# Two-block transformer on one core: three weight tiles of the second token tile fetched during the first, and the order of the expert-row slots

## The reference

```python
# end of the first block
h = rms_norm(x, norm_ffn_g[l]) * (1.0 + sc2) + sh2
x = x + gt2 * (jnp.square(jax.nn.relu(h @ ffn_w1[l])) @ ffn_w2[l])
# second block
h = h + hybrid_mixer(rms_norm_2(h, norm_mix_g[l]), w_in[l], ...)
h = h + peer_ffn(rms_norm_2(h, norm_ffn_g[l]), w_peer_q[l], ...)
# peer_ffn, per token: the rows of 8 x 16 experts
hval = jnp.einsum('cd,chkd->chk', xc, expert_u[ic])
a = gc * jax.nn.gelu(hval, approximate=False)
y = jnp.einsum('chk,chkd->cd', a, expert_v[ic])
```

## Time and profile before

| | |
|---|---|
| median of 3 runs | 1539.07 us (1538.23 to 1541.64) |
| profiled execution, its own time | 1537.54 us |
| its span | 1536.2 us |
| TensorE busy | 1236.7 us, 81% of the span |
| VectorE busy | 937.5 us, 61% |
| ScalarE, GpSimd busy | 395.7 us (26%), 378.5 us (25%) |
| bytes moved | 488.51 MB, of these 268.45 MB by the gathers (q0), 215.55 MB by SP's queue (q1) |
| chain that ended last | TensorE 45%, DMA 28%, DVE 17% |

### The profile page before, as it was taken

The page is one execution under the profiler, slowest core; times in us unless marked ns, Lnnn a source line. Parts: engine busy times, 40 slices in busy tenths (PEclk is TensorE's granted clock), DMA queues, the critical chain, the costliest instruction groups (busy, mean ns, idle before and its releaser), DMA issues.

```text
span 1536.2 us, 14325 instructions
## 1 busy us (share of the span) xinstructions
PE 1236.7 (81%) x4974; PEld 764.9 (50%) x4974; DVE 937.5 (61%) x2022; ACT 395.7 (26%) x1043; POOL 378.5 (25%) x285
## 2 busy tenths in 40 slices
PE   2989999979999899877777756786489777788775
PEld 2875555654676685477445454433284332333332
DVE  6278877945111221156766779998668777767653
ACT  2162111121100222112212132343214433333322
POOL 0001121200000000023333323434237544444430
PEclk9999999979999898987888879879689999989999
DMA  9633334525588665749999999999999999999995
GB/s 365 242 145 123 124 136 165 195 108 190 233 333 342 228 260 188 285 187 422 424 424 424 424 420 422 366 389 423 401 358 387 421 421 421 421 420 422 420 422 218
DMA packets 56233, 488.51 MB, mean 318 GB/s; under 512 B 6496, under 2 KB 8800, under 8 KB 10080
## 3 DMA queue, kind: packets, MB, share of 16 engines
q0 software_dynamic: 36864, 268.45, 42.4%
q1 hardware_dynamic: 18144, 215.55, 35.9%
q10 hardware_dynamic: 1152, 3.59, 0.6%
HBM read 486.51 MB, written 1.05 MB: 317 GB/s over the span
## 4 chain that ended last, share of the span: by engine, by line
PE 45%; DMA 28%; DVE 17%; issue 4%; ACT 3%; POOL 2%; another core or an unknown queue 0%; ACTq 0%; DVEq 0%; SPq 0%
PE ps L452 24%; DMA arena<-in_euv,arena 18%; PE ps L855 7%; DMA ring<-in_w 7%; PE ps L529 6%; PE ps L816 5%; DVE xr L1736 3%; DVE arena L1712 2%; DVE arena L1043 2%; PE ps L982 1%; DVE arena L1306 1%; POOL arena L2247 1%; DVE arena L1313 1%; DMA ring<-in_g 1%; DMA ring<-in_pq 1%
## 5 line engine op out<-in xcount | busy, mean ns | idle before, releaser
L2247 POOL DMA_INDIRECT arena<-in_euv,arena x163 | 216.4, 1328 | 615.5 <-DVE arena L1706 331.6
L452 PE MATMUL ps<-arena,ring 128*128 128x128 f32 (+1 forms) x2320 | 317.5, 301 | 39.0 <-DVE arena L1080 9.8
L452 PEld LDWEIGHTS ps<-arena,ring 128*128 128x128 f32 x2320 | 304.7, 204 | 59.1 <-DVE arena L1074 10.9
L1712 DVE CUSTOM_DVE_ANT_0 arena<-arena 128x1024 f32<-128x1024 f32 x163 | 197.5, 1220 | 61.4 <-DMA arena<-in_euv,arena 60.9
L982 PE MATMUL ps<-arena 128*128 128x512 f32 x356 | 171.3, 629 | 41.1 <-ACT arena L2148 41.1
L855 PE MATMUL ps<-ring,arena 128*128 128x512 f32 x256 | 127.2, 656 | 35.8 <-DMA ring<-in_w 35.8
L982 PEld LDWEIGHTS ps<-arena 128*128 128x128 f32 x356 | 68.7, 199 | 141.5 <-issue 76.2
L452 PE MATMUL ps<-arena 128*128 128x128 f32 (+4 forms) x684 | 114.1, 315 | 26.2 <-ACT arena L1806 19.8
L816 PE MATMUL ps<-ring,arena 128*128 128x512 f32 x256 | 122.3, 630 | 11.3 <-DVE arena L1074 9.1
L982 PE MATMUL ps<-ring,arena 128*128 128x512 f32 x216 | 106.7, 636 | 28.7 <-ACT arena L2148 28.7
L2157 ACT ACTIVATE arena<-arena 128x2 f32<-128x2 f32 x128 | 25.9, 203 | 402.3 <-DVE arena L1712 397.4
(11 more groups left out here) (304 smaller groups left out, 1235.6 us busy)
## 6 DMA issues: line engine op xcount, KB each, us to landing
ring<-in_w SPq DMA_DIRECT2D x32, 2048.0 KB, 8.4
ring<-in_ada SPq DMA_DIRECT2D x12, 2048.0 KB, 13.4
ring<-in_qkv SPq DMA_DIRECT2D x12, 2048.0 KB, 7.6
ring<-in_gates SPq DMA_DIRECT2D x8, 2048.0 KB, 7.6
ring<-in_g SPq DMA_DIRECT2D x8, 2048.0 KB, 7.7
ring<-in_pq SPq DMA_DIRECT2D x8, 2048.0 KB, 7.6
ring<-in_wp SPq DMA_DIRECT2D x5, 2048.0 KB, 7.7
ring<-in_wout SPq DMA_DIRECT2D x4, 2048.0 KB, 7.6
```

What stands on the lines that cost most here:

```text
L452: ins = te.matmul(o, l, r, start=(i == 0), stop=(i == len(pairs) - 1))
L1712: ins = v.tensor_tensor_reduce(out=x, in0=x, in1=xn[:, tt, :], scale=1.0, scalar=0.0, op0=ALU.mult, op1=ALU.add, accum_out=hv[:, n % 16:n ...
L2247: gp.indirect_dma_start(slots[i], None, A["euv"], bass.IndirectOffsetOnAxis(ap=idx[:, n // 16 % 4, e % 16:e % 16 + 1].bitcast(U32), axis=0 ...
```

## The change

Three things are changed.

1. The first five weight tiles of token tile 1 get places of their own: `w1 0` and `w1 1` in buffers 0 and 1, `w2 0` in buffer 2, `w1 2` and `w2 1` in two new places `ahead`, which are the arena's row slots. From the sixth tile on, two buffers are used in turn. The two tiles in `ahead` are fetched just before tile 0's `qkv 0` and `qkv 3`.
2. The slots join the line later. The line begins with five (4, 7, 8, 9, 10): `arena[0:2048]`, `K`, the one over `hT`, and two that are lent by the score buffer `pexp` and by `keys`. At row 9 the two halves of ring buffer 2 join, when `w2 0` has been used; at row 13 and row 17 two each of the `ahead` places, when `w1 2` and `w2 1` have been used. From row 36 on the two lent slots are left out, until row 114. One arena slot is gone for good: 16 in all at the end instead of 17.
3. Three engines' waits say that the lent slots have been given back before attention writes there.

```diff
-SPOT = [n % RING if n < SECOND else (n - SECOND) % 2 for n in range(len(STREAM))]
+SPOT = [n % RING if n < SECOND else n - SECOND if n < SECOND + 5 else (n - SECOND - 5) % 2 for n in range(len(STREAM))]
+
+AHEAD = {("qkv", 0, 0): SECOND + 3, ("qkv", 3, 0): SECOND + 4}
...
+JOINS = (9, 13, 17)
+LEAVE = 36
...
+        if n == LEAVE:
+            line = [i for i in line if i not in lent]
         i = line.pop(0)
...
-        slots = [area(2 * D) for _ in range((ARENA + D - top[0]) // (2 * D) - 1)]
+        ahead = [arena[:, top[0] + i * TILE:top[0] + (i + 1) * TILE] for i in range(2)]
+        slots = [area(2 * D) for _ in range(4)]
         slots += [arena[:, 0:2 * D], ring[:, 2, 0:2 * D], ring[:, 2, 2 * D:4 * D], K[:, K_SU:K_SU + 2 * D]]
-        slots += [arena[:, ARENA - D:ARENA + D]]
+        slots += [arena[:, ARENA - D:ARENA + D], f4(pexp), keys]
...
-        slot_of, turn_of = row_slots(range(n_early), {2 * AMONG + 10: list(range(n_early, len(slots)))})
+        lent = (9, 10)
+        joins = {JOINS[0]: [5, 6], JOINS[1]: [0, 1], JOINS[2]: [2, 3],
+                 2 * AMONG + 10: [*range(n_early, len(slots)), *lent]}
+
+        weights_at = {5: SECOND + 2, 6: SECOND + 2, 0: SECOND + 3, 1: SECOND + 3, 2: SECOND + 4, 3: SECOND + 4}
+        slot_of, turn_of = row_slots((4, 7, 8, *lent), joins, lent)
...
                     if tt and i == 0:
-                        v.wait_ge(*full("sc0.3"))
+                        v.wait_ge(*returned(9))
...
+                    if tt and kind == 0 and c == 0:
+                        sc.wait_ge(*returned(10))
...
                 if i in last:
                     gp.wait_ge(*slot_done[last[i]])
+                    if i in lent and last[i] < LEAVE <= n:
+                        gp.wait_ge(*full("sc1.3"))
+                elif i in weights_at:
+                    gp.wait_ge(*spent[STREAM[weights_at[i]]])
                 elif i < n_early:
-                    gp.wait_ge(*full("sc0.3" if i == n_early - 1 else "sc0.0"))
-                    gp.wait_ge(*spent[STREAM[[m for m in range(SECOND) if SPOT[m] == 2][-1]]])
+                    gp.wait_ge(*full("sc0.0" if i < 8 else "sc0.3"))
...
+                if key in AHEAD:
+                    late_key = STREAM[AHEAD[key]]
+                    sy.wait_ge(sig("xn"), NORMED["f1"])
+                    sy.dma_start(weights(*late_key), A[late_key[0]][late_key[1]]).then_inc(loaded(*late_key)[0], 16)
+                if n in AHEAD.values():
+                    continue
```

More of the change, by code:

```diff
@@ L212, in on_vector, with row_slots @@
     return n < 2 * AMONG
-def row_slots(first, later):
+JOINS = (9, 13, 17)
+LEAVE = 36
+def row_slots(first, later, lent):
     line, slot, nth, seen = list(first), [], [], {}
@@ L378, in build @@
         diag = area(N_DIAG, 128)
-        slots = [area(2 * D) for _ in range((ARENA + D - top[0]) // (2 * D) - 1)]
+        ahead = [arena[:, top[0] + i * TILE:top[0] + (i + 1) * TILE] for i in range(2)]
+        slots = [area(2 * D) for _ in range(4)]
         slots += [arena[:, 0:2 * D], ring[:, 2, 0:2 * D], ring[:, 2, 2 * D:4 * D], K[:, K_SU:K_SU + 2 * D]]
         assert top[0] <= ARENA - D
-        slots += [arena[:, ARENA - D:ARENA + D]]
+        slots += [arena[:, ARENA - D:ARENA + D], f4(pexp), keys]
         n_early = len(slots)
         slots += [ring[:, r, j * 2 * D:(j + 1) * 2 * D] for r in range(2) for j in range(2)]
-        slots += [f4(pexp), keys, kT2.rearrange("p a b c -> p (a b c)")]
-        slot_of, turn_of = row_slots(range(n_early), {2 * AMONG + 10: list(range(n_early, len(slots)))})
+        slots += [kT2.rearrange("p a b c -> p (a b c)")]
+        lent = (9, 10)
[3 more added lines that the diff above has]
+        slot_of, turn_of = row_slots((4, 7, 8, *lent), joins, lent)
         def gathered(n):
@@ L393, in build, with returned @@
         slot_done = {}
+        def returned(i):
+            return slot_done[max(n for n in range(LEAVE) if slot_of[n] == i)]
         pools = {"main": (0, 1, 2, 3), "misc": (4, 5, 6, 7), "s5": (2, 3, 7)}
@@ L419, in weights @@
         def weights(*key):
-            return ring[:, SPOT[PLACE[key]], :]
+            i = SPOT[PLACE[key]]
+            return ring[:, i, :] if i < RING else ahead[i - RING]
         def loaded(*key):
@@ L2093, in late @@
                     sc.wait_ge(*full(name))
+                    if tt and i == 0:
+                        sc.wait_ge(*returned(10))
                     emptied(sc.activation(sg2[:, i % 2, :], psum(name)[:], ACT.Sigmoid), name)
```

## The result

| | before | changed |
|---|---|---|
| median | 1538.48 us (1534.35 to 1542.63, 10 runs) | 1547.45 us (1545.32 to 1553.58, 10 runs) |
| ratio | | 1.0057, 95% interval 1.0043 to 1.0071 |
| span of the profiled execution | 1536.2 us | 1551.6 us |

The change makes the kernel 8.8 us slower (the ratio's distance from 1, times 1538 us; the interval is 6.6 to 10.9 us). The forecast was +2 us, a median of 1541.0 us, "no change, by a hair's breadth slower". The result is 6.4 us above it. It lies inside the whole range, 1531.5 to 1552, but outside the forecast's own range of -3 to +6 us (1536 to 1545): the upper part of the whole range came from the rivals B and C, and neither of them is what happened, as will be seen. That the range holds is luck.

The account below looks back on a forecast made before the run. DMA engines were taken as the bound: rows and tiles share them full from 700 to 880 us, rows alone from 1157. Terms -3 + 0 + 5 = +2 us gave 1541.0 us; own range 1536 to 1545, whole range 1531.5 to 1552.

Parts of the forecast that it names:

- B: Slower rival: the 5.68 us gap near 688 us stays, rows lag 13.0 us, about 1549 us; chance 0.22.
- C: Slower rival: rows and tiles share DMA evenly, 4.95 us a row over 22 rows, +8.6 us, about 1550; chance 0.13.
- Part 1: Full DMA stretch behind 681 us: two early tiles take 4.19 MB out of it, -9.9 us if bytes alone counted.
- The cover for the early tiles: Tile 0: delayed `qkv` loads have the feed-forward layer's end and norm over them, cost nothing; uncovered, up to 5 us each.
- Part 2: Start of the rows: two gathers go out instead of nine before `sc0.3`, full at 700.1 us; lag 2.25 MB, +5.3 us.
- the pause: Unexplained 5.68 us before ACT's copy at 694.03 us, amid nine gathers; expected gone with two.
- Part 3: Stretch up to tile 1's last `x1`: row 41 at 871.8 us, second half at about 876 against 878.77, -3 us.
- Part 4: Attention stretch: nine slots instead of ten from row 43 on cost 0; bounds -5 and +5 us.
- Part 5: Handover at rows 113 and 114: issues restart 3.3 us later, one row less under way; two rows missing, +5.0 us.
- A: Faster rival: the bytes win, row 41 arrives before the two `qkv` tiles; -4 to -8 us, about 1533; chance 0.25.
- D: Rival inside the forecast: third tile brings no bytes, neither `x1` nor handover costs over one row; +2.5 us; 0.40 with forecast.
- my own sign: Tile 1's second `x1` instruction: near 876 us the forecast, near 869 A, past 882 B or C.

Follow-up runs that it names:

- late_tiles: Changed kernel, but `w1 2` and `w2 1` fetched in stream order, behind 681 us, not during tile 0: +21.7 us against the kernel before (four launches).
- before_two_early: Kernel before, with only the first two gathers allowed ahead of `sc0.3`, the other eight slots waiting for it: +8.9 us against the kernel before.
- hold_qkv: Changed kernel, but SP may not fetch `qkv 0` of token tile 1 before row 41 has arrived: +0.9 us against the kernel before.
- join_113: Changed kernel, but the slots that come free with `sc1.3` join at row 113, not row 114: +4.5 us against the kernel before.
- all_three: Changed kernel with its given-up arena slot back, `w2 0` fetched ahead of `w1 0`, and `qkv 0` held until row 41: 1527.54 us, -11.7 us against before.
- w20_first: Changed kernel, but SP fetches `w2 0` of token tile 1 ahead of `w1 0`: +4.2 us against the kernel before.

## Why the prediction was right in part, and where it was not

**Part 1, the bytes: right.** Putting the two tiles back behind 681 us moves row 41 by 9.6 us in the profile (late_tiles), forecast 9.9. The cover for the early tiles held, to 0.2 us.

**Part 2, the start: right in its numbers, its reason open.** I expected the pause to go because it lay in the middle of the burst of nine gathers. It went, but it is also gone with eight, so the burst as such is not its cause, and the guess was in part luck. With it, `sc0.3` was full 7.0 us sooner (forecast 7.5), and the 19 us from the first gather on had 4.83 MB (forecast 4.7). The DMA view of the changed kernel from 686 to 705 us, against the earlier trace rows:

```profile
DMA packets 583, 4.83 MB, mean 254 GB/s; under 512 B 64, under 2 KB 64, under 8 KB 192
```

Over the whole stretch up to row 41 the lag can be read from two windows. Before it is 681 to 869 us, then 686 to 879 us of the changed kernel:

```profile
DMA packets 8526, 78.47 MB, mean 417 GB/s; under 512 B 937, under 2 KB 937, under 8 KB 1065
```
```profile
DMA packets 8483, 78.14 MB, mean 405 GB/s; under 512 B 935, under 2 KB 935, under 8 KB 1063
...
q0 software_dynamic: 6025, 43.93, 55.1%
q1 hardware_dynamic: 2448, 34.08, 42.1%
```

At 424 GB/s these take 185.1 and 184.3 us; the rest is idle, 2.9 and 8.7 us. The difference, 5.8 us, is the lag that I put at 5.3. In the old kernel a start with two gathers cost `x1` 10.6 us (before_two_early), so the 5.3 holds only for the two starts with their tiles as they are here.

**Part 3, the last `x1`: the step that failed.** Forecast -3 us, measured +4.2. Two terms of it were mis-sized, the first by 2.8 us and the second by 4.2, which makes the 7.0 us by which the second half of `x1` is late (forecast 876, measured 883.0 by the old clock).
- The `qkv` tiles. SP's queue had 34.08 MB in both windows: what the two early tiles took out, the two `qkv` tiles put back, whole. I counted one and a half of them, 7.4 us; it was two, 9.9. With that, row 41 would be at 869 + 5.3 - 9.9 + 9.9 = 874.3 us by the old clock. By the packets of the gathers it was there 193.4 us behind the first gather, or 874.6, where I had 871.8. The run that holds the two back (hold_qkv) brings it 9.9 us sooner, to 183.5.
- From row 41 to `x1`. I let DVE stand ready when row 41 arrives, and gave 4.2 us from there. But the last row that DVE waited for was 39. From its dot product at 876.21 DVE works through to 888.07, 11.9 us, and row 41 arrives in the middle. From the dot product of row 40 to the second `x1` half it is 7.34 us when nothing waits (hold_qkv: 876.80 to 884.14), since the adds of the group before and the dot product of row 41 stand between. From row 41's arrival it was 8.4 us, not 4.2. That is the larger part of the miss.

**Part 4, attention: right.** Forecast 0; from `x1` to row 103 262.8 us against 263.4, and the old kernel with nine slots 263.5. The profiles of all kernels lie between 259.4 and 263.5 us, so a pair alone would not show so small a difference; that nine slots cost nothing rests on the old kernel's two profiles, which agree within 0.2 us up to row 103.

**Part 5, the handover: right mechanism, too small.** Forecast +5.0; measured +6.7 behind row 103 in the changed kernel and +7.2 in the old kernel with nine slots. I put POOL's wait at 3.3 us and rounded wait and missing row to two rows. They add in full: 4.2 us for the wait (join_113) and 2.6 for what is left, near one row. The wait itself was 4.6 us, from `sc1.3` at 1166.6 to the gather at 1171.20.

**The rivals.** A, the bytes win, needed row 41 ahead of the `qkv` tiles: it did not come by itself, and it comes when forced (hold_qkv, all_three). B is out, since the pause went; yet its lag of 13 us warned of what a late start can cost. By my own sign, `x1` past 882 us, it had to be B or C, and at 883.0 it was neither: the sign was no test of them. D is out, since both `x1` (+4.2) and the handover (+6.7) moved. C is out as well. From 800 to 879 us the engines were full and the rows got this:

```profile
DMA packets 3586, 33.47 MB, mean 424 GB/s; under 512 B 398, under 2 KB 398, under 8 KB 398
...
q0 software_dynamic: 2575, 18.75, 57.1%
q1 hardware_dynamic: 1008, 14.68, 43.7%
```

18.75 MB are 17.9 rows in 79 us, 4.4 us each, not 4.95. The 14.68 MB of SP's are seven tiles; at an even share, 9.9 us each, they fill 69 of the 79 us, so SP still had pauses in which the rows had the engines alone (an estimate from these rows). The rule of the Trainium skill ("DMA: Bandwidth & Descriptors", section "Queues, rings and completion order"), turns by packet between queues that have work, is neither shown nor contradicted by this, since SP did not always have work. The even share that I drew from it did not come. It also took the two queues' packets to be of one size; those that the trace counts are not: SP's held 14.6 KB in the mean (14.68 MB in 1008) and the gathers' 7.3 KB (18.75 MB in 2575).

The sum by the profile: +4.2 - 0.6 + 6.7 = +10.3 us, where the forecast had -3 + 0 + 5 = +2. The medians say +8.8.

## What to carry to other kernels

Taking bytes out of a full stretch helps only if nothing takes their place: the engine that gains a lead fetches the next tiles, and they pass the rows that are now late. Where two queues share the DMA engines, tie the transfer that is not yet needed to the arrival of the one that is. And in a queue that issues strictly in order, look at whose release the first instruction behind a change of regime needs: one slot fewer turned a fast release into a slow one and held up seven free slots behind it.

## What the runs showed of the hardware

**Launches differ ahead of any change.** The first gather came between 681.0 and 689.7 us in kernels that are the same up to there, or differ only in early tile loads. The cause is not shown. Single spans were therefore no measure of these changes; times behind a common event were, and medians.

**The attention stretch differs between profiles, in part by the granted clock.** From `x1` to row 103 the profiles took 259.4 to 263.5 us. One step can be seen in sixteen matmuls of one form, first in the timeline and the windows of the kernel before:

```profile
1057.47 8.80 PE L452 MATMUL ps<-ring,arena 128*128 128x512 f32 x16 [1.92 <-issue]
```
```profile
core 0: us, PE busy (x) PEld busy (x) DVE busy (x) ACT busy (x) POOL busy (x), PEclk, DMA share, GB/s
1057.40:1066.30 8.90, 8.80 (x16) 3.53 (x16) 4.81 (x6) 3.83 (x6) 3.47 (x3) 0.81 1.01 425
```

and then in those of the old kernel with seven early gathers:

```profile
1057.47 7.03 PE L452 MATMUL ps<-ring,arena 128*128 128x512 f32 x16
```
```profile
core 0: us, PE busy (x) PEld busy (x) DVE busy (x) ACT busy (x) POOL busy (x), PEclk, DMA share, GB/s
1045.00:1052.00 7.00, 6.26 (x10) 3.35 (x11) 6.76 (x17) 5.74 (x12) 4.00 (x3) 0.51 1.03 435
...
1057.40:1064.60 7.20, 7.10 (x17) 2.85 (x15) 4.38 (x6) 3.85 (x6) 3.05 (x3) 1.00 1.02 428
```

The first ran partly at the lower level, 1.2 GHz (mean 0.81), the second wholly at 2.4 GHz (1.00), and that is 1.8 us. The second kernel had its 0.51, the lower level, before, from 1045 to 1052 us, where the first had 1.00: its dip fell on other work. So 1.8 us in these matmuls go with the granted clock. The whole stretch is 3.3 us shorter in the second kernel (260.1 and 263.4 us); what the rest comes from is not shown.

**A gather behind queued tiles.** Row 2 of the changed kernel, issued at 706.07, 2 us behind two tile fetches, took 12.70 us on the chain. With `w2 0` fetched sooner (w20_first), and so only one tile just ahead of it, the same piece took 9.37 us, 3.3 us less. So this late gather paid for the tiles queued just ahead of it.
